# Moving the four transposes of the first feed-forward tiles from the first to the second accumulation pass of the tile after them

## The reference

```
def swiglu(x, w_in, w_out):
    gate, up = jnp.split(x @ w_in, 2, axis=-1)
    return (jax.nn.silu(gate) * up) @ w_out
...
h = h + 0.5 * rmsnorm(swiglu(rmsnorm(h, g[0]), ffn1_w_in[i], ffn1_w_out[i]), g[1])
...
h = h + 0.5 * rmsnorm(swiglu(rmsnorm(h, g[4]), ffn2_w_in[i], ffn2_w_out[i]), g[5])
```

## Time and profile before

| | |
|---|---|
| time, median of 3 runs | 1448.14 us (1446.93 to 1448.79) |
| the profiled execution's own time | 1447.81 us |
| its span, first to last instruction | 1446.0 us |
| TensorE busy | 1412.0 us, 98% of the span |
| VectorE / ScalarE busy | 959.4 us (66%) / 748.6 us (52%) |
| weights loaded by SyncE's queue | 261.65 MB, 49.3% of the DMA engines' time |
| mean granted TensorE clock | 0.994 |

### The profile page before, as it was taken

The page is one execution under the profiler, slowest core; times in us unless marked ns, Lnnn a source line. Parts: engine busy times, 40 slices in busy tenths (PEclk is TensorE's granted clock), DMA queues, the critical chain, the costliest instruction groups (busy, mean ns, idle before and its releaser), DMA issues.

```text
span 1446.0 us, 18169 instructions
## 1 busy us (share of the span) xinstructions
PE 1412.0 (98%) x7038; PEld 1187.3 (82%) x7038; DVE 959.4 (66%) x917; ACT 748.6 (52%) x787; POOL 75.2 (5%) x91
## 2 busy tenths in 40 slices
PE   7999999999999999999999989999999999999997
PEld 6888888777888888878888868888888878788886
DVE  6869686775775766776774775774774546577636
ACT  4674665545553457654543554543544445455524
POOL 0000000010000200110000110000202101000001
PEclk9999999999999999999999999999999999999999
DMA  9746444564555543463555373555463633545541
GB/s 393 290 156 265 182 178 152 179 235 173 194 184 195 200 186 118 159 228 136 195 186 229 131 276 132 182 196 219 161 229 118 221 128 145 220 153 196 190 189 44
DMA packets 40388, 272.62 MB, mean 189 GB/s; under 512 B 4609, under 2 KB 5505, under 8 KB 8706
## 3 DMA queue, kind: packets, MB, share of 16 engines
q1 hardware_dynamic: 36864, 261.65, 49.3%
q10 hardware_dynamic: 3458, 10.04, 2.0%
HBM read 270.62 MB, written 1.05 MB: 188 GB/s over the span
## 4 chain that ended last, share of the span: by engine, by line
PE 89%; DVE 6%; DMA 2%; ACT 2%; issue 1%; POOL 1%; SPq 0%; ACTq 0%; DVEq 0%; POOLq 0%
PE acc L2181 18%; PE acc L2484 18%; PE acc L2183 18%; PE acc L2182 18%; PE acc L2485 9%; DVE wlo L1235 3%; PE turn L2234 3%; ACT whi L431 1%; DMA mod_raw<-in_units 1%; DMA gpost<-in_norm_g 1%; PE aux L2758 0%; PE turn L2383 0%; PE aux L2309 0%; PE aux L2632 0%; DMA gpost<-in_g_final 0%
## 5 line engine op out<-in xcount | busy, mean ns | idle before, releaser
L1235 DVE TENSOR_TENSOR wlo<-raw,whi 128x2048 fp32r<-128x2048 f32 x233 | 532.8, 2296 | 152.4 <-ACT whi L431 152.1
L431 ACT ACTIVATE whi<-raw 128x2048 fp32r<-128x2048 f32 x233 | 445.0, 1915 | 225.7 <-PE acc L2183 150.5
L2484 PE MATMUL acc<-feeds,whi 128*128 128x512 f32 x1152 | 406.5, 397 | 0.0
L2181 PE MATMUL acc<-whi,feeds 128*128 128x512 f32 (+1 forms) x888 | 354.5, 399 | 4.2 <-DVE wlo L1235 4.2
L2183 PE MATMUL acc<-whi,feeds 128*128 128x512 f32 (+1 forms) x888 | 345.8, 389 | 0.0
L2182 PE MATMUL acc<-wlo,feeds 128*128 128x512 f32 (+1 forms) x888 | 345.2, 389 | 0.0
L2485 PE MATMUL acc<-feeds,wlo 128*128 128x256 f32 x1152 | 323.9, 281 | 0.0
L2484 PEld LDWEIGHTS acc<-feeds,whi 128*128 128x128 f32 x1152 | 218.3, 190 | 50.4
L2485 PEld LDWEIGHTS acc<-feeds,wlo 128*128 128x128 f32 x1152 | 219.5, 191 | 0.2
L2181 PEld LDWEIGHTS acc<-whi,feeds 128*128 128x128 f32 x888 | 167.6, 189 | 41.9 <-DVE wlo L1235 6.8
L2183 PEld LDWEIGHTS acc<-whi,feeds 128*128 128x128 f32 x888 | 167.3, 188 | 35.4
(11 more groups left out here) (358 smaller groups left out, 1107.7 us busy)
## 6 DMA issues: line engine op xcount, KB each, us to landing
raw<-in_units SPq DMA_DIRECT2D x237, 1024.0 KB, 4.8
mod_raw<-in_units SPq DMA_DIRECT2D x6, 1024.0 KB, 11.0
gpost<-in_norm_g ACTq DMA_DIRECT2D x8, 512.0 KB, 4.5
gpre<-in_norm_g ACTq DMA_DIRECT2D x6, 512.0 KB, 4.9
mod_more<-in_units SPq DMA_DIRECT2D x2, 1024.0 KB, 23.5
h<-in_x SPq DMA_DIRECT2D x2, 512.0 KB, 10.4
w_ax<-in_w_ax SPq DMA_DIRECT2D x1, 1024.0 KB, 26.5
bgate<-in_b_gate SPq DMA_DIRECT2D x1, 1024.0 KB, 27.8
```

Of the source, the lines that this page charges most:

```text
L431: act.activation(whi[:, u % RING, :], raw[:, u % RING, :], ACT.Copy).then_inc(hi_ready, 1)
L1235: dve.tensor_tensor(wlo[:, u % RING, :], raw[:, u % RING, :], whi[:, u % RING, :].bitcast(F32), ALU.subtract).then_inc(lo_ready, 1)
L2181: pe.matmul(out, xh, wh, start=first, stop=False)
L2484: pe.matmul(both, whi[:, s, w], feeds[:, :, kc, :], start=kc == 0, stop=False)
```

## The change

On TensorE the hook is called ahead of half 1 of pass 1 instead of pass 0; `hidden(1)` then asks for the same count of `acc_free[1]` as before (the argument `back` takes off the one that `ready(1)` has added meanwhile). On ScalarE and VectorE the evacuation of pass 0 of tile 2 (`tile_rest(0)`, `tile_sum(0)`) moves ahead of the copies of the transposed values (`hidden(1)`). ScalarE gets one wait more, for `mul(0)` to have read `sgl`.

```
 (ScalarE)
                 silu(1)
+                act.wait_ge(acc_free[0], n["e"][0])
+                tile_rest(0)
                 hidden(1)
-                tile_rest(0)
                 tile_done(FF_FIRST)
...
 (VectorE)
                 mul(1)
+                tile_sum(0)
                 hidden(1)
                 dve.wait_ge(moved[row_moved[0]], row_moved[1])
-                tile_sum(0)
                 tile_done(FF_FIRST)
...
 (TensorE)
-                def hidden(t):
-
-                    pe.wait_ge(acc_free[t], n["e"][t])
+                def hidden(t, back=0):
+
+                    pe.wait_ge(acc_free[t], n["e"][t] - back)
                     turns([hid[:, t, c // 2, P * (c % 2):P * (c % 2) + P] for c in range(4)])
...
                         for half in range(2):
-                            if half and not c and hook is not None:
+                            if half and c and hook is not None:
                                 hook()
...
-                tile(hook=lambda: hidden(1))
+                tile(hook=lambda: hidden(1, back=1))
```

## The result

The changed kernel takes 1436.61 us (median of 6 runs, 1435.73 to 1436.81) against 1447.54 us for the kernel before (6 runs, 1445.60 to 1448.79): a ratio of 0.9925, 95% interval 0.9912 to 0.9938. That is 10.9 us less, where 16.3 were forecast. The profiled execution took 1436.81 us with a span of 1434.9 us, 11.1 us less than before.

A forecast was written before the change was run, and what follows sets the result against it. TensorE, busy for 98% of the span, was taken as the bound. Four passes 0 of 41.30 us become 4 x (5.58 + 0.17 + 0.50) = 25.0 us: gain 16.3 us, time 1431.8 us, range 1429.8 to 1435.8 us.

The forecast's parts named there:

- the stall: TensorE's wait for `mul(1)` before the transposes in pass 0 of tile 2, rooted in VectorE's queue: 2.82 us idle per part.
- Pass 0 of tile 2 without hook and stall: Pass 0 of tile 2, 10.29 us in the second part, would last 5.58 us once the hook leaves it.
- The transposes in pass 1: The four transposes cost 0.50 us per part in pass 1 as in pass 0, bounds 0.41 to 0.77.
- The wait at `ready(1)`: At the start of pass 1, a new short wait for `mul(1)` costing 0.17 us a part, bounds 0.05 to 0.63.
- the slow stretch: Matmuls at lower clock behind the idle time in pass 0, 5.7 us over four parts, would go with it.
- The lists on ScalarE and VectorE: The new order costs nothing: `hi(u8)` begins about 0.9 us later against TensorE, hidden by 3.4 us of slack.
- Gain 16.3 us: Four passes 0 of 41.30 us become 25.0 us with wait and transposes; all carried into the span, time 1431.8 us.
- Rival A: Idle time before the transposes goes but the clock falls all the same: gain 10.6 us, time 1437.5 us; 8%.
- B: The new wait at `ready(1)` costs 0.63 us a part: gain 14.5 us, time 1433.7 us; 8%.
- C: Gain hidden: TensorE enters the tile loop early and waits there for weights no earlier than before: 1448 us; 2%.
- D: Slower: `hi(u8)` behind the copy of the transposes makes weights late: slower by 2.9 us, 1451 us; 1%.
- the page's penalty: Half the throttled time lost behind an idle gap: 1.68 us a part, giving gain 17.3 us and time 1430.8 us.

The follow-up runs named there:

- e1: The kernel before with only TensorE's part of the change (transposes in pass 1), ScalarE and VectorE as before: 1435.95 us, ratio 0.9909.
- e3: The changed kernel with a fifth transpose at the hook, repeating the fourth into the same place: 1435.11 us in one run.
- e11: The changed kernel run again, unchanged: 1436.35 us (4 runs).
- e4: The changed kernel with the hook moved ahead of half 0 of pass 1, between the passes: 1434.54 us in one run.
- e5: The kernel before, unchanged, profiled a second time: 1449.80 us.
- e6: The kernel of e4 with the stall put back by extra VectorE writes of a weight's low part ahead of `mul(1)`: 1450.42 us, ratio 1.0016.
- e9: The kernel before with its pairs of matmuls in the order 512, 512, 256, 256 columns: 1446.82 us, ratio 0.9988.
- e7: The changed kernel with its pairs of matmuls in the order 512, 512, 256, 256 columns: 1431.09 us, ratio 0.9880.

## Why the prediction was right or wrong

What bounds the kernel, the place and the root of the stall: right. The wait went, and in its place came only the short one at `ready(1)`.

Pass 0 of tile 2 without hook and stall: 5.58 us forecast, 5.64 found. The transposes in pass 1: 0.50 forecast; found 0.43, from the two intervals around them (0.706 and 0.433 us against 0.353 for each). The wait at `ready(1)`: 0.17 forecast, 0.09 found (0.442 against 0.353 us). Together with pass 1 the sum was 25.0 + 4 x 5.55 = 47.2 us, and 47.20 were measured. That it fits so closely is luck: the transposes and the wait were put 0.15 us a part too high, and the 32 pairs of the two passes, at the slow pace, as much too low. That the slow stretch goes with the stall: right, the mean clock is 0.999. The lists on ScalarE and VectorE: `hi(u8)` begins at 650.80, 1.13 us behind the end of half 0 of pass 1 where 1.2 were forecast, and ends 0.42 us before `tile_rest(1)` where 0.3 were; `lo(u8)` begins 2.84 us behind the end of tile 2, against 2.77 before.

The step that failed is the one behind the sum, the time of tiles 3 to 10, whose change was put at nothing and measured 5.1 us: "Gain 16.3 us" was taken over into the span with the sentence that all four parts pay, "since TensorE has no wait of its own for a weight inside them that could swallow the time". I took the 5.55 us of the undisturbed pass for a constant of the kernel. It was the pace of one stream behind one stall. Two things in the trace of before spoke against it. The first eight pairs of pass 0 went at 0.351 us a pair, which is the slow pattern, in all four parts; I used the number and did not ask about it. And pass 1 of the third part took 5.65 us, which I did not look at. The runs show in its place a pace of two values, 0.3467 and 0.3533 us, which can change where the stream is interrupted and holds from the last interruption for some 90 us.

How often the fast pace came depends on the kind of interruption. Counted from start to start over the nine profiles with the old order of pairs:

| the stream of pairs starts | fast pace behind it |
|---|---|
| at the beginning of tile 2 | 0 of 36 |
| behind the short wait at `ready(1)` (changed kernel, e1, e3, e11) | 10 of 16 |
| behind the transposes at full clock, with no wait or one of at most 0.5 us (changed kernel, e1 to e4, e11) | 2 of 24 |
| behind the transposes and a stall of 2.7 to 2.9 us, clock not fallen (e5, e6) | 0 of 3 |
| behind such a stall, where the clock fell and rose again (before, e5, e6) | 6 of 9 |

In the kernel before, the last event ahead of the loop was the rise of the clock; in the changed one it is the transposes. So the change did not slow anything by itself: it left the loop behind an event after which the fast pace is rare. That a restart at the lower clock makes the fast pace likelier is what these counts suggest; e5 had three falls and one fast loop, so it is no rule. DMA traffic does not sort the loops: the DMA share was 0.53 to 0.56 in the stretches at the fast pace and 0.50 to 0.55 in those at the slow one.

Rival A had a time near the measured one (1437.5 us), but for another reason: its fall of the clock did not happen. The slow pace is no lower clock; the granted clock is 1.00 in every stretch. B had the right place and the wrong size, C and D did not come about.

With the pace held equal the forecast can be tested as it stood: e9 and e7 differ only by the change, and by 15.7 us, where 16.3 were forecast; a single missing fall of the clock, as in e9's profile, would account for the 0.6 us between and more. The spread of the runs fits too: 3.2 us in the first six runs of before, 1.1 us after.

The Trainium skill, "TensorE: Matmul & The Clock Gate", section "HAM oscillation — how this bites in real kernels", has a burst behind an idle gap start at half clock. Of 16 stalls of 2.7 to 2.9 us in the profiles (before, e5, e6, e9) 12 were followed by a fall and 4 were not. The gain that the prediction worked out with the page's penalty, 17.3 us, is further off than the 16.3 from start-to-start times: 16.4 were measured in tile 2. The trace shows one reason why that penalty, half of the time at the lower clock, is too high here: a pair took 0.640 us there and 0.347 to 0.353 at the full clock, less than twice as long.

What stays open is the mechanism of the pace. The trace shows a hitch of some 11 ns in every third pair, with 2 to 3 ns more in the two others, and that the order of long and short matmuls changes it; which part of TensorE is out of step with which is not visible in it. Whether the fast pace can be brought about on purpose was not settled: e3 and e4 hit it in one loop each, in one run each.

## What to carry to other kernels

When a stall is taken away, the streams behind it are not a constant: compare their pace, from start to start and in several places, before a gain is carried to the end of the span. Where a kernel repeats the same loop several times, look at each of them in the trace of before; one that differs is a question to be asked before predicting. And an alternation of long and short matmuls is worth trying in another order: two and two gave back here what the removal of the stall had lost, 5.5 us. In the kernel before, half of whose profiled loops were fast, the same order brought only 1.9 us (e9).

## What the runs showed of the hardware

- A stream of alternating 512- and 256-column matmuls, each with its own weight load, ran at 0.3467 or at 0.3533 us a pair, both at full clock and with no wait, and held the value for all of 8 tiles (256 pairs), across the turns of a loop.
- The pace changed only at interruptions: behind a wait that cost 0.09 us it came out fast 10 times of 16, behind four or five transposes at full clock 2 times of 27. One program took different paces in two executions (before and e5), and a difference of 4 to 5 ns in the length of an interruption went with the other pace once (e4).
- In the order 512, 512, 256, 256 it was 0.3483 us a pair in 8 of 8 profiled loops without a stall and 4 of 4 with one; four long and four short gave 0.3508 or 0.3500.
- Of 16 idle gaps of 2.7 to 2.9 us in a dense stream, 12 were followed by a stretch at 1.2 GHz that cost 1.3 to 1.6 us, and 4 by none. In that stretch a pair of the old order took 0.640 us.
